# A transformer layer's mixer on one core: matmul operands halved to f16 in rows and turned by DMA instead of by TensorE

## What is computed

```python
def reference(x, meta_tokens, rel_bias, ...):
    h = jnp.concatenate([meta, x], axis=1)
    hn = rms_norm(h, mix_norm_g[l])
    proj = hn @ w_in[l]
    q, k, v, cb, cc, ch = jnp.split(proj, SPLITS, axis=-1)
    q = rms_norm(q.reshape(bsz, seq, N_Q_HEADS, HEAD_DIM), q_norm_g[l])
    k = rms_norm(k.reshape(bsz, seq, N_KV_HEADS, HEAD_DIM), k_norm_g[l])
    a = sliding_window_sink_attention(q, k, v, attn_sinks[l], rel_bias)
    c = short_gated_conv(cb, cc, ch, conv_w[l])
    mixed = jnp.concatenate([rms_norm(a, attn_out_norm_g[l]), rms_norm(c, conv_out_norm_g[l])], axis=-1)
    h = h + mixed @ w_out[l]
    hn = rms_norm(h, ffn_norm_g[l])
    return (h + hierarchical_moe(hn, ...))[:, N_META:]
```

## Time and profile before

| | |
|---|---|
| median of three runs | 2934.0 us (2933.37 to 2936.19) |
| the profiled execution: device time, span | 2933.6 us, 2932.0 us |
| mixer, to the first expert instruction | 1500.3 us |
| experts | 1431.7 us |
| PE busy in the whole span | 2833.6 us, 97% |
| mean granted TensorE clock | 0.986 of full speed |

### The profile page before, as it was taken

One profiled execution on the slowest core, in us unless ns is written; L12 is line 12 of the kernel. 1 busy time (PEld: TensorE's weight loads), 2 busy tenths in 40 slices (PEclk: granted clock), 3 DMA queues, 4 the chain that ended last, 5 costly groups with the idle time before them and its releaser, 6 DMA issues. The chain is left out here.

```text
span 2932.0 us, 51902 instructions
## 1 busy us (share of the span) xinstructions
PE 2833.6 (97%) x15862; PEld 2015.1 (69%) x15863; DVE 1685.4 (57%) x4102; ACT 1424.0 (49%) x3174; POOL 809.2 (28%) x826
## 2 busy tenths in 40 slices
PE   4999999999999999999859999999999999999998
PEld 2565566556556656655538888888888888888886
DVE  5566666666666666666643546645564545356543
ACT  6655454555455455545423445544454444345433
POOL 1122223313222221321212323323322323333222
PEclk9899999999999999999979999999999999999999
DMA  8112112111211211221335667766776756657763
GB/s 291 40 69 79 57 61 79 66 63 68 79 53 65 79 64 57 75 78 50 140 111 162 183 196 222 237 200 195 233 243 194 229 150 197 180 170 232 241 189 57
DMA packets 152747, 398.52 MB, mean 136 GB/s; under 512 B 18027, under 2 KB 18188, under 8 KB 151692
## 3 DMA queue, kind: packets, MB, share of 16 engines
q1 hardware_dynamic: 123868, 309.36, 30.6%
q0 software_dynamic: 28848, 88.77, 13.0%
HBM read 310.20 MB, written 87.88 MB: 136 GB/s over the span
## 5 line engine op out<-in xcount | busy, mean ns | idle before, releaser
L412 PE MATMUL psG<-wi_all,xT_hi 128*128 128x512 f16 x1024 | 308.1, 383 | 0.7 <-DVE xT_lo L944 0.7
L1333 PE MATMUL psB<-up_hi,gT_hi 128*128 128x512 f32 x632 | 254.2, 402 | 0.0
L1333 PE MATMUL psA<-gate_hi,gT_hi 128*128 128x512 f32 x632 | 246.6, 390 | 3.1 <-ACT gT_hi L1453 1.7
L1333 PE MATMUL psB<-up_hi,gT_lo 128*128 128x512 f32 x632 | 247.4, 391 | 0.0
L1257 POOL DMA_INDIRECT xg<-hn_rows,slots x80 | 98.2, 1228 | 539.7 <-DMA slots<-slot_table 394.2
L1333 PE MATMUL psA<-gate_hi,gT_lo 128*128 128x512 f32 x632 | 246.7, 390 | 0.0
L1333 PE MATMUL psA<-gate_lo,gT_hi 128*128 128x512 f32 x632 | 246.3, 390 | 0.0
L1333 PE MATMUL psB<-up_lo,gT_hi 128*128 128x512 f32 x632 | 246.2, 390 | 0.0
L1469 DVE TENSOR_TENSOR down_lo<-wi_all,down_hi 128x512 fp32r<-128x512 f32 x256 | 157.0, 685 | 147.3 <-ACT down_hi L1427 147.3
L1453 ACT ACTIVATE gT_hi<-psC 128x512 fp32r<-128x512 f32 x80 | 47.8, 598 | 383.1 <-PE psC L1341 383.1
L1483 DVE TENSOR_TENSOR act_rows<-psB,gated 128x512 f32<-128x512 f32 x79 | 54.7, 692 | 289.6 <-PE psB L1333 289.6
(11 more groups left out here) (343 smaller groups left out, 7174.9 us busy)
## 6 DMA issues: line engine op xcount, KB each, us to landing
wi_all<-in_w_gate SPq DMA_DIRECT2D x32, 2048.0 KB, 9.4
wi_all<-in_w_up SPq DMA_DIRECT2D x32, 2048.0 KB, 12.8
wi_all<-in_w_down SPq DMA_DIRECT2D x32, 2048.0 KB, 9.2
xt<-in_x SPq DMA_DIRECT2D x32, 512.0 KB, 3.3
um<-u_rows SPq DMA_DIRECT2D x64, 256.0 KB, 2.7
xres<-in_x SPq DMA_DIRECT2D x32, 512.0 KB, 4.1
out_rows<-h SPq DMA_DIRECT2D x32, 512.0 KB, 2.6
hn_rows<-hn SPq DMA_DIRECT2D x32, 512.0 KB, 2.6
```

What stands on the lines that cost most here:

```text
L412: m = nc.tensor.matmul(ps, left[l][:, k, :], weights.half(r, k, n, width), start=(k == 0 and j == 0), stop=(k == KD - 1 and j == 2))
L1333: m = nc.tensor.matmul(ps[:, :], l[:, k, :], r[:, r_k[n], :], start=(n == 0 and j == 0), stop=(n == len(l_k) - 1 and j == 2))
```

## The change

Every operand is now halved where it lies in rows, in SBUF. ACT writes `hi` as f16, DVE writes `lo` as f16, and SP then has the DMA engines turn both halves from SBUF to SBUF (`dma_start_transpose`, in `turn`). PE has no transposes left. The scores take f16 queries and keys in place of fp32r ones (a query tile holds hi and lo side by side in its 128 columns, as before). Norm factors are folded into the halving (`halve`).

The output projection, and the residual and norm after it, of tile t move from `body(t)` to `body(t+1)`. The router of a tile keeps its body, and the counting and listing of its experts moves one body later. `schedule` calls one more body, t = 34. Several buffers now share memory: `m16` (halves of a and yc) lies in `prob`, the halves of hn lie in `a` and `Cs`, and `hn` lies in `xres`. Each sharing adds a wait.

```diff
+        def turn(signal, t, places, source, ready):
+            seen(*ready)
+            sp.dma_start_transpose(places, source).then_inc(signal.sem, 16)
...
+            if proj:
+                seen(ph, t)
+                seen(pb, t)
+                turn(xT_in, t, both_xT[:, 0], x16[:, 0], (x_hi_s, t + 1))
+                turn(xT_in, t, both_xT[:, 1], x16[:, 1], (x_lo_s, t + 1))
...
+            if attn:
+                seen(o_ps, t - 1)
+                for g in range(2):
+                    half = slice(g * D, (g + 1) * D)
+                    for side, done in enumerate((p_hi, p_lo)):
+                        turn(probT_in[g], t, both_probT[:, side, 4 * g:4 * g + 4].rearrange("p h c q -> p (h c) q"),
+                             prob16[:, side, half], (done, t, g + 1))
...
+            if attn:
+                turn(mT_in, t, both_mT[:, 0, 0:4], m16[:, 0, 0:CC], (a_hi, t))
+                turn(mT_in, t, both_mT[:, 1, 0:4], m16[:, 1, 0:CC], (a_lo, t))
...
             if attn:
-                after(pe, qT_act, t)
-                after(pe, kT_s, t)
+                after(pe, qT_in, t)
+                after(pe, kT_in, t)
...
+            if res:
+                after(pe, mT_in, t - 1)
+                after(pe, h_s, t - 2)
+                split_mm(psE[:, :], both_mT, "out", 0, new_out).then_inc(h_ps.sem, 1)
+                split_mm(psF[:, :], both_mT, "out", 512, new_out).then_inc(h_ps.sem, 1)
...
-            if attn:
-                for j, ps in enumerate((psA, psB, psC, psD)):
-                    after(pe, p_sb, t, 2 * j + 2)
-                    for i in range(4):
-                        hd, c = 2 * j + i // 2, i % 2
-                        m = nc.tensor.transpose(ps[:, i * P:(i + 1) * P], prob[:, hd, c * P:(c + 1) * P], ident)
...
+        def halve(signal, t, source, junk, ss, ln, r, rx, width, upper, done):
+            s.activation(junk, source, ACT.Square, accum_out=ss).then_inc(signal.sem, 1)
+            after(act, signal, t, 1)
+            rstd(signal, t, ss, ln, r, width, 1)
+            after(act, signal, t, 3)
+            s.activation(rx, r, ACT.Copy, scale=XS).then_inc(signal.sem, 1)
+            after(act, signal, t, 4)
+            s.activation(upper, source, ACT.Copy, scale=rx).then_inc(done.sem, 1)
...
+                for g in range(2):
+                    part = slice(g * D, (g + 1) * D)
+                    after(dve, p_hi, t, g + 1)
+                    v.scalar_tensor_tensor(prob16[:, 1, part], prob_flat[:, part], PS, prob16[:, 0, part],
+                                           ALU.mult, ALU.subtract).then_inc(p_lo.sem, 1)
```

More of the change, by code:

```diff
@@ L320, in schedule @@
             body(t)
-        for t in range(TILES - 1, TILES + 2):
+        for t in range(TILES - 1, TILES + 3):
             body(t)
@@ new lines, in body @@
+            if new_in:
+                for k in range(KD):
+                    pe.wait_ge(v_sq, k + 1)
+                    m = nc.tensor.matmul(psG[:, 0:P], cst[:, C_ONE:C_ONE + P], w_sq[:, k, :], start=(k == 0), stop=(k == KD - 1))
+                m.then_inc(v_cols, 1)
+            if full:
+                after(pe, c_sb, t)
+                after(pe, s_sb, t)
+                split_mm(psC[:, :], both_xT, "in", O_C).then_inc(pc.sem, 1)
+            if attn:
+                after(pe, v_cur, t)
+                after(pe, s_sb, t)
+                for hd in range(HEADS):
+                    if hd % 4 == 0:
+                        after(pe, probT_in[hd // 4], t)
+                    kv, ps, at = hd // 4, (psA, psB)[hd // 4], hd % 4 * P
+                    for c, half in ((0, 0), (0, 1), (1, 1), (1, 0)):
+                        m = nc.tensor.matmul(ps[:, at:at + (P, HD)[half]], both_probT[:, half, hd, c, :],
+                                             V[:, c, kv, 0:2 - half, :].rearrange("p a d -> p (a d)"),
+                                             start=(c == 0 and half == 0), stop=(c == 1 and half == 0))
+                m.then_inc(o_ps.sem, 1)
@@ L474, in body @@
+            if full:
+                after(pe, u_s, t)
+                split_mm(psD[:, :], both_xT, "in", O_H).then_inc(ph.sem, 1)
+            if res:
+                after(pe, hnT_in, t - 1)
+                if proj:
+                    after(pe, k_n, t + 1)
+                    after(pe, v_st, t + 1)
+                after(pe, rt2, t - 2)
+                after(pe, counted, t - 2)
                 for k in range(KD):
@@ L818, in body @@
                 g.tensor_tensor(yc[:], yc[:], Bs[:], ALU.mult).then_inc(cv.sem, 1)
+            if count:
+                after(pool, rt2, t - 2)
+                hold(pool, held)
+                for n in range(2):
+                    g.indirect_dma_start(table, bass.IndirectOffsetOnAxis(ap=slot[:, n:n + 1], axis=0),
+                                         entry[:, n, :], None, bounds_check=E * CAP - 1).then_inc(listed.sem, 16)
             if proj:
```

704 lines of the change are left out of this document (312 added, 392 removed).

## The result

The changed kernel took a median of **2779.12 us** (2776.05 to 2781.87), the kernel before, on the same chip, 2933.97 us (2933.37 to 2936.19). The ratio is 0.9471, with a 95% interval from 0.9454 to 0.9487. The forecast was 2789 us.

A forecast was written before the change was run, and what follows sets the result against it. PE's cycles per tile were taken to bound the mixer loop. From 2933.6 us, -175 (31 periods), -10 (moved output projection), +5 (start) and +35 (tail) make -145: 2789 us, range 2765 to 2815.

The forecast's parts named there:

- PE bounds the loop, and 5.64 us per tile go: Mixer loop: without 50 turns (5.47 us) and with cheaper scores (0.17), a tile goes from 42.96 to 37.3 us.
- No other engine becomes the bound: Mixer loop: DVE's 28 and ACT's 23 us per tile grow by about 2 each and stay under 37.3.
- Turns of about 1 us of the DMA engines per 256 KB: SP's DMA queue: 11.5 turns of 256 KB per tile at about 1 us each, beside 7.7 us of plain DMAs.
- the room of 2.6 us: SP's DMA queue: the most a 256 KB turn may take before transfers exceed PE's tile, (37.3 - 7.7) / 11.5.
- The share of 0.4: Sign of a right forecast: DMA engines busy about 0.4 of the time in the loop.
- SP issues a turn in 0.8 us: SP's queue: 14 turns per tile at 0.8 us take 11 us of SP's 37.
- Each operand is covered by at least 2.4 us: Mixer loop: each landing hides behind PE work; tightest is a, 5.7 us of slack against about 3.3 needed.
- Rival 1: Mixer loop: the DMA queue becomes the bound above 2.6 us per 256 KB, slower from about 3, up to 3895 us; chance 0.22.
- Rival 2: Output projection: a's turns take 8 us, 2.3 too late per tile, 2860 us; chance 0.13 with a partly late queue.
- Start and first periods: Up to tile 32's scores: -175 over 31 periods, -10 for the moved output projection, +5 for early waits.
- The tail, +35: From tile 32's scores to the experts: exposed turns, work order and clock add 18, 10, 4 and 3 us; range 20 to 50.
- Experts unchanged: Expert phase after the mixer: no change in its time.

The follow-up runs named there:

- four small turns: Changed kernel with four constant 128x128 turning DMAs added on SP's queue ahead of the turns of a and yc: 2927.75 us.
- experiment 2: Changed kernel with three or six plain 1 MB copies from SBUF to HBM per tile added on SP's queue inside the loop: 2776.73 and 2916.88 us.
- Experiment 7: Changed kernel with the first expert's three 2 MB loads moved from ahead of tile 32's turns to one body later: 2769.54 us.

## Why the prediction was right, step by step

- **PE bounds the loop, and 5.64 us per tile go.** Right in the mechanism: 37.32 us against a forecast 37.3, and putting the 50 turns back returns 5.45 of it. PE's list of waits in the loop is empty.
- **No other engine becomes the bound.** Right. In 10.7 tiles DVE has 309 us and ACT 231, that is 28.8 and 21.6 us per tile, against forecasts of about 30 and 25.
- **Turns of about 1 us of the DMA engines per 256 KB.** The term was too small. 0.66 x 37.32 is 24.6 us per tile, less 7.7 for the plain DMAs is 16.9, by 11.5 is about **1.47 us**, if the plain DMAs cost what they did before; that is twice a plain copy's 0.7. The bounds (0.7 to 5.7) held it and the room of 2.6 us hid it. The share of 0.4 that the prediction expected does not follow from its own term either: (7.7 + 11.5) / 37.3 is 0.51. The Trainium skill's 261 GB/s ("DMA: Bandwidth & Descriptors", Latency and other measured facts) gives 1.0 us, an estimate; the 1.47 us measured here are 178 GB/s. The Trainium skill's 1309 ns for one 128x128 of bf16 ("VectorE: DVE Perf Modes", The three transpose paths) is near the 1.23 us that SP's issue of one takes here, but eight squares in one turn take the same issue and not eight times it: 3.2 us to landing for 256 KB, 2.4 for 32 KB.
- **SP issues a turn in 0.8 us.** Too small: 1.19 to 1.30 us in the medians. Fourteen are 17 us of SP's 37, not 11. That was free, since SP had room, but it is what made a's place tighter.
- **Each operand is covered by at least 2.4 us.** Right in its consequence, wrong in its size and in the place. For `a`: the second turn is issued by 658.19, and where PE did wait for it, it started 1.3 us after the issue's end (four small turns). That makes 659.5 against PE's need at 661.35: 1.8 us. The margin that ends first was not in my list: `both`, 0.3 to 0.6 us, on a chain from `um` through POOL, ACT and DVE. I had followed each turn to its reader, and not what stands behind the turns in SP's queue.
- **Rival 1.** Didn't come true. It begins where the engines are full; experiment 2 puts that between 0.92 and 1.02 of share. One sum of it was wrong: at 2.95 us, 31 x 1.4 us is 43 us and still pays for the 30 at the ends; the two are even at 42.0 us per tile, 2.98 us per 256 KB. The 2.8 us per 256 KB that it lets SP's queue hold has no working.
- **Rival 2.** Didn't come true, by a margin far smaller than I thought: one issue of 1.2 us more in SP's queue costs 0.41 us per tile. With four small turns its price was also more than the wait: 3.3 us of PE's idle time per tile and 1.5 more, with the granted clock at 0.96 in the loop.
- **Start and first periods.** I had -180 at tile 32's scores, with +5 for the start. It was -186.1. Tile 2's scores already came 20.9 us earlier, where 5.64 + 10 - 5 makes 11, and the next three periods, of 38.4 us in the mean, gave 3 back, 2.7 of it in two waits of PE (for `both_mT` and `both`). The +5 had the wrong sign. Nearly all of the 20.9 lies between the scores of tiles 1 and 2:

```profile
99.69:154.84 55.15, 55.15 (x285) 30.31 (x284) 28.86 (x61) 27.49 (x65) 15.89 (x14) 0.88 0.17 59
```

```profile
97.97:133.93 35.96, 35.69 (x186) 17.13 (x185) 24.07 (x52) 24.28 (x57) 9.01 (x8) 0.91 0.44 99
```

The work that leaves this stretch is 10.4 + 5.6 us. The clock lost 6.8 us in it before and 3.4 now: 3.4 more. That makes 19.4 us, where 19.2 were measured. PE does wait once for a turn, 11.2 us for `both_xT`, but ahead of the scores of tile 1, which come 1.7 us earlier all the same.
- **The tail, +35.** Right in kind, 6 too large: +28.8. The part up to PV was +15.1 (24.1 against 9.0) where I had +18; the part after it 62.3 against 48.5 us, +13.8, where I had +17. Experiment 7 shows that the expert loads ahead of the turns are the cause of 12 of the first.
- **Experts unchanged.** +5.6 in these two profiled runs. Nothing in the change touches them, and in the traces of the twelve other kernels, whose experts are the same too, this phase took between 1432.1 and 1438.8 us. So the 5.6 is within what such runs differ by from one another.

So the two errors of the ends, 6 each, added up to 12 on the fast side, and the experts took 5.6 back: 2789 - 12 + 5.6 is about 2782, the profiled run. That the total came within 10 us of the forecast is in part luck; the loop's period is not.

## What to carry to other kernels

Where one engine is busy all the time and the DMA engines are not, moving its transposes to them gave back its cycles here, as long as every operand stayed on time. Count the engines' share, the queue's issue time, and the slack of the nearest reader, in this order. For the slack, follow not only the DMA that is added but each one queued behind it, through every in-order engine that waits for it, back to the bound engine. At the end of this pipeline the turns were exposed, and there the bulk loads did better behind them in the queue.

## What the hardware did that I had not expected

- The issue of a turning DMA cost 1.23 us for 32 KB, 1.2 for 128 KB, 1.25 for 256 KB and 2.40 for 512 KB (medians), where a plain one costs 0.35. With the DMA engines full it took up to 5.1, and behind three loads of 2 MB the first took 9.87.
- With PE idle for 3.3 us in all between the scores and the output projection of every tile the granted clock in the loop was 0.96, and 3.5 us of added work in that place made the kernel 17 us faster at 1.00. As much idle time in three shorter waits per tile left it at 1.00.
- The DMA engines took a share of 0.92, at 243 GB/s with turns and copies mixed, and no operand was late.
